# In block 2 and its FFN, h is made without 1/rms and the products are scaled on GpSimd

## The reference, cut to what matters

```
x = first_block(...)                      # ends: x = rmsnorm(x, final_norm_g)
h = x * rsqrt(mean(x*x) + 1e-6) * norm1_g
p = h @ w_in                              # columns: u 1024, v 1024, g 1024, x_lru 1024
u, v = gelu(p_u), layernorm(gelu(p_v))
y_gm = u * (tril(ws) @ v + bs)            # per chunk of 128 tokens and head
y_lru = rg_lru(causal_conv4(p_x)) * gelu(p_g)
x = x + concat(rmsnorm(y_gm), rmsnorm(y_lru)) @ w_out
h = x * rsqrt(mean(x*x) + 1e-6) * norm2_g
up = causal_conv3(h @ ffn_w_up)           # 2048 -> 12288 columns
x = x + (gelu(up_gate) * up_val) @ ffn_w_down
return rmsnorm(x, final_g)
```

## Time and profile before

| | us |
|---|---|
| median of 3 runs (lowest to highest) | 2453.39 (2450.84 to 2458.06) |
| the profiled execution | 2454.96 |
| its span | 2453.2 |
| mean granted clock of TensorE | 0.978 |
| TensorE, products busy | 2324.8 (95%) |
| VectorE busy | 1291.5 (53%) |
| ScalarE busy | 1043.2 (43%) |
| GpSimd busy | 197.1 (8%) |

### The profile page before, as it was taken

One profiled execution on the slowest core, in us unless ns is written; L12 is line 12 of the kernel. 1 busy time (PEld: TensorE's weight loads), 2 busy tenths in 40 slices (PEclk: granted clock), 3 DMA queues, 4 the chain that ended last, 5 costly groups with the idle time before them and its releaser, 6 DMA issues.

```text
span 2453.2 us, 30580 instructions
## 1 busy us (share of the span) xinstructions
PE 2324.8 (95%) x12135; PEld 1861.9 (76%) x12135; DVE 1291.5 (53%) x2110; ACT 1043.2 (43%) x1596; POOL 197.1 (8%) x237
## 2 busy tenths in 40 slices
PE   5889999999999979899989988989999999999998
PEld 2467777677777657678877867868888888888887
DVE  2444533142332263545666776557665676567664
ACT  2232333342321263445544545445543555345543
POOL 1000100000010131100021014120000000000001
PEclk8999999999999999999989999989999999999999
DMA  9864433335655565534555554646655655565652
GB/s 367 294 236 172 142 120 124 123 112 171 232 172 172 202 221 208 167 102 147 187 157 171 180 172 130 189 132 186 189 181 188 189 183 186 186 186 186 188 184 83
DMA packets 347021, 436.66 MB, mean 178 GB/s; under 512 B 13848, under 2 KB 269280, under 8 KB 345984
## 3 DMA queue, kind: packets, MB, share of 16 engines
q1 hardware_dynamic: 341376, 413.19, 51.8%
q0 software_dynamic: 3408, 16.38, 1.9%
q10 hardware_dynamic: 2096, 5.15, 0.6%
HBM read 428.37 MB, written 6.29 MB: 177 GB/s over the span
## 4 chain that ended last, share of the span: by engine, by line
PE 85%; DVE 5%; ACT 4%; DMA 3%; issue 2%; POOL 1%; SPq 0%; ACTq 0%; POOLq 0%; DVEq 0%
PE ps L1151 32%; PE ps L1152 16%; PE ps L1146 5%; PE ps L1148 5%; PE ps L1147 5%; PE ps L1132 4%; PE ps L1134 4%; PE ps L1133 4%; PE ps L1113 3%; ACT SPL L1329 2%; DVE SPL L1555 2%; PE ps L1196 1%; PE ps L1213 1%; DMA RAW<-in_w_in_dram 1%; DMA RAW<-in_ada_w_dram 1%
## 5 line engine op out<-in xcount | busy, mean ns | idle before, releaser
L1151 PE MATMUL ps<-HS,SPL 128*128 128x512 f32 x3456 | 1236.1, 402 | 16.9 <-POOL HS L2007 16.1
L1555 DVE TENSOR_TENSOR SPL<-RAW,SPL 128x1024 fp32r<-128x1024 f32 x592 | 726.4, 1233 | 669.4 <-ACT SPL L1329 667.3
L1152 PE MATMUL ps<-HS,SPL 128*128 128x256 f32 x3456 | 973.6, 282 | 0.0
L1329 ACT ACTIVATE SPL<-RAW 128x1024 fp32r<-128x1024 f32 x592 | 621.7, 1057 | 536.1 <-PE ps L1152 356.5
L1151 PEld LDWEIGHTS ps<-HS,SPL 128*128 128x128 f32 x3456 | 654.6, 189 | 183.4 <-POOL HS L2007 16.9
L1152 PEld LDWEIGHTS ps<-HS,SPL 128*128 128x128 f32 x3456 | 658.2, 190 | 2.1 <-issue 1.9
L1132 PE MATMUL ps<-SPL,HS 128*128 128x512 f32 x576 | 248.5, 431 | 30.1 <-ACT XT L1371 8.5
L1134 PE MATMUL ps<-SPL,HS 128*128 128x512 f32 x576 | 228.5, 397 | 0.0
L1133 PE MATMUL ps<-SPL,HS 128*128 128x512 f32 x576 | 228.4, 396 | 0.0
L1146 PE MATMUL ps<-HS,SPL 128*128 128x512 f32 x512 | 212.2, 414 | 1.2 <-DVE HS L1711 1.2
L1148 PE MATMUL ps<-HS,SPL 128*128 128x512 f32 x512 | 200.5, 392 | 0.0
(11 more groups left out here) (251 smaller groups left out, 1543.7 us busy)
## 6 DMA issues: line engine op xcount, KB each, us to landing
RAW<-in_w_in_dram SPq DMA_DIRECT2D x208, 512.0 KB, 5.6
RAW<-in_ada_w_dram SPq DMA_DIRECT2D x192, 512.0 KB, 4.9
RAW<-in_ffn_w_up_dram SPq DMA_DIRECT2D x192, 512.0 KB, 3.6
RAW<-in_w_out_dram SPq DMA_DIRECT2D x96, 512.0 KB, 4.5
RAW<-in_ffn_w_down_dram SPq DMA_DIRECT2D x96, 512.0 KB, 3.4
x_spill<-XT POOLq DMA_DIRECT2D x2, 2048.0 KB, 14.8
XT<-x_spill POOLq DMA_DIRECT2D x1, 4096.0 KB, 15.8
MM<-in_x_dram ACTq DMA_DIRECT2D x2, 1024.0 KB, 10.8
```

The source lines that it names most:

```text
L1151: mm(PS[b][:, :], wr, hh, start=k == 0, stop=False, skip_group_check=True)
L1152: m = mm(PS[b][:, 256:512], wl, hh[:, 0:256], start=False, stop=k == KT - 1, skip_group_check=True)
L1329: act(SPL[:, (n - 1) % NSPL, 0, :], raw_of(i), ACT.Copy).then_inc(s_hi, 1)
L1555: tt(w[:, 1, :], raw_of(s["i"]), w[:, 0, :].bitcast(F32), ALU.subtract).then_inc(s_lo, 1)
```

## The change

For the h of block 2 and of the FFN the 1/rms is left out. `bare_tile` takes the place of `split_tile`: two tiles are put into `hi` as soon as an out group has summed them, the high part by ScalarE from x times g, the low part by VectorE. The norm's steps become steps of `hi` during the first group of the next projection: `both_a` (count, means, power, diagonals), `both_b` (rows), `keep_rows`, which copies the rows into SBUF (RSB) and at the first seam two columns (VRS); `up_a`, `up_b`, `keep_rows` at the second. The planner pops `hi` until the rows are there (`kept`) before it puts the first join. After each join of u, x_lru, g and the FFN's up groups GpSimd multiplies the two joined tiles by RSB (`join_scale`), and the consumer waits for that; the Gelu of v takes 1/rms as its scale per token. `keep_x` waits for the tile of h made from the same x. The product of the two channel weights (`gain_both`) is made ahead of layer 2's out projection.

```diff
@@ join
-        def join(outs, banks, done):
+        def join(outs, banks, done, rows=None):
             s = put("join", outs=outs, banks=banks, last=done)
             ready = [(s_jd, 2 * s["n"] - 1), (s_jd, 2 * s["n"])]
             for b, r in zip(banks, ready):
                 bank_last[b] = [r]
+            if rows is None:
+                return ready
+            z = put("join_scale", outs=outs, ready=ready, rows=rows)
+            y["rows_read"] = (s_js, 2 * z["n"])
+            return [(s_js, 2 * z["n"] - 1), (s_js, 2 * z["n"])]
+
+        def bare_tile(k, src, g, dst, ready, done, last):
+            z = {}
+            def s0():
+                z["n"] = put("bare_hi", src=src, g=g, dst=dst, last=[ready, *last])["n"]
+            def s1():
+                done[k] = (s_bl, put("bare_lo", src=src, g=g, dst=dst, hi=z["n"])["n"])
+            return [s0, s1]
+
+        def made(done):
+            def ready(k):
+                while k not in done:
+                    hi.pop(0)()
+                return [done[k]]
             return ready
+
+        def keep_rows(ready, after):
+            s = put("keep_rows", last=[ready, *after])
+            bank_last[5] = [(s_rsb, s["n"])]
+            y["rows"] = (s_rsb, s["n"])
+
+        def kept():
+            while "rows" not in y:
+                hi.pop(0)()
+            return y["rows"]
@@ x_out (layer 2); x_add the same with "if squares is sq2"
+                    if not both:
+                        hi.extend(staged([y["tile"](j0 + i, (s_res, n + i)) for i in range(2)]))
@@ u_out; xlru_out, g_out and up_out the same
-                ready = join([UU[:, j0 + i, :] for i in range(2)], banks, [multiplied(), y["ended"]])
+                ready = join([UU[:, j0 + i, :] for i in range(2)], banks, [multiplied(), y["ended"]], kept())
@@ first seam
-        y["ended"] = add_up1(marks[4])
...
-        need["in2"] = on_demand([split_tile("in", k, XV[:, 0, k, :], GG[:, k, :], RS0, HH[0][:, k, :, :], lambda: [(s_bnr, 1), (s_gg1, 1)],
-                                            done, [y["ended"]]) for k in range(KT)], done)
-        need["in2"](1)
+        put("gain_both")
+        done_in = {}
+        read_in = multiplied()
+        y["tile"] = lambda k, ready: bare_tile(k, XV[:, 0, k, :], GG[:, k, :], HH[0][:, k, :, :], ready, done_in, [read_in, (s_gg1, 1)])
+        run_chunks(marks[4])
+        y["ended"] = multiplied()
...
+        need["in2"] = made(done_in)
         put("lru_maps_in", last=[y["ended"]])
-        hi.extend([idle] * 2 + [keep_x(k) for k in range(KT)] + [lambda: put("decay")])
+        hi.extend([both_a, idle, both_b, lambda: keep_rows((s_bnr, 1), [])] + [keep_x(k) for k in range(KT)] + [lambda: put("decay")])
@@ second seam
-        flush(hi)
         y["down"] = multiplied()
...
+        hi.extend([up_a, idle, up_b, lambda: keep_rows(y["up_rows"], [read])])
@@ ScalarE
+                    act(s["dst"][:, 0, :], s["src"], ACT.Copy, scale=s["g"]).then_inc(s_bh, 1)
...
-                        act(VN[:, t, s["g"] * 512:(s["g"] + 1) * 512], PS[b][:, :], ACT.Gelu_apprx_tanh).then_inc(s_vc, 1)
+                        act(VN[:, t, s["g"] * 512:(s["g"] + 1) * 512], PS[b][:, :], ACT.Gelu_apprx_tanh, scale=VRS[:, t:t + 1]).then_inc(s_vc, 1)
@@ VectorE
+                elif kind == "bare_lo":
+                    e.wait_ge(s_bh, s["hi"])
+                    stt(s["dst"][:, 1, :], s["src"], s["g"], s["dst"][:, 0, :].bitcast(F32), ALU.mult, ALU.subtract).then_inc(s_bl, 1)
+                elif kind == "keep_rows":
...
+                    if n == 1:
+                        copy(VRS, RSTD[:, 2:4])
+                    copy(RSB, RS0).then_inc(s_rsb, 1)
@@ GpSimd
+                elif kind == "join_scale":
...
+                    for o, (sm, v) in zip(s["outs"], s["ready"]):
+                        e.wait_ge(sm, v)
+                        tt(o, o, RSB, ALU.mult).then_inc(s_js, 1)
```

More of the change, by code:

```diff
@@ L794, in f @@
             def f():
-                need["in2"](k)
-                s = put("keep_x", k=k, last=[(s_bnr, 2)])
+                s = put("keep_x", k=k, last=[(s_bnr, 2), done_in[k]])
                 bank_last[4] = [(s_kx, s["n"])]
@@ L810, in f @@
                 pads = (s_z, s["n"])
-                ready = join([T(a)[:, 3:259], T(b)[:, 3:259]], banks, [multiplied(), *la, *lb])
+                ready = join([T(a)[:, 3:259], T(b)[:, 3:259]], banks, [multiplied(), *la, *lb], kept())
                 z = {}
@@ L852, in f @@
             def f():
-                s = put("v_gelu", g=g, banks=banks, last=[multiplied()])
+                s = put("v_gelu", g=g, banks=banks, last=[multiplied(), kept()])
                 for i, b in enumerate(banks):
@@ L882, in f @@
                 xs = [T(slot)[:, 0:256], T(slot)[:, 256:512]]
-                ready = join(xs, banks, [multiplied(), *last])
+                ready = join(xs, banks, [multiplied(), *last], kept())
                 def mul():
@@ L901, in f @@
                         squares.add(XV[:, 0, j0 + i, :], j0 + i, (s_res, n + i))
+                if squares is sq2:
+                    hi.extend(staged([y["tile"](j0 + i, (s_res, n + i)) for i in range(2)]))
             return f
@@ L911, in f @@
                 cs = [c0, (c0 + 1) % 8]
-                ready = join([CV[c][:, 2:258] for c in cs], banks, [multiplied(), (s_pad, 1), *conv_last[cs[0]], *conv_last[cs[1]]])
+                ready = join([CV[c][:, 2:258] for c in cs], banks, [multiplied(), (s_pad, 1), *conv_last[cs[0]], *conv_last[cs[1]]], kept())
                 ks = (2 * i, 2 * i + 1)
@@ L1000, in two_block_program, with both_a, both_b @@
         project1(marks[3])
-        y["ended"] = add_up1(marks[4])
[L1004 to L1010, removed]
-        need["in2"] = on_demand([split_tile("in", k, XV[:, 0, k, :], GG[:, k, :], RS0, HH[0][:, k, :, :], lambda: [(s_bnr, 1), (s_gg1, 1)],
-                                            done, [y["ended"]]) for k in range(KT)], done)
-        need["in2"](1)
+        put("gain_both")
[4 more added lines that the diff above has]
+        y["ended"] = multiplied()
+        def both_a():
+            sq1.count(6)
+            cnt = sq1f.count(6, 2)
+            y["both_slot"], last = take()
+            y["power"] = tick("power")
+            put("both_norms", slot=y["both_slot"], last=[cnt, *last], power=y["power"])
+            bank_last[6] = [(s_bn, 1)]
+        def both_b():
+            put("both_rows", slot=y["both_slot"], after=use(4, 5))
+            give(y["both_slot"], (s_bnr, 2))
+        need["in2"] = made(done_in)
         put("lru_maps_in", last=[y["ended"]])
-        hi.extend([idle] * 2 + [keep_x(k) for k in range(KT)] + [lambda: put("decay")])
+        hi.extend([both_a, idle, both_b, lambda: keep_rows((s_bnr, 1), [])] + [keep_x(k) for k in range(KT)] + [lambda: put("decay")])
         run_chunks(marks[5])
@@ L1044, in two_block_program, with up_a, up_b @@
         run_chunks(marks[8])
-        flush(hi)
         y["down"] = multiplied()
-        cnt = sq2.count(4)
-        slot, bank_last[4] = rstd_a(2, 1.0 / D, PS[4][:, 0:2], [cnt])[0], [(s_ms, count["rstd_a"])]
-        rs2 = rstd_b(2, slot, 5)
-        done2 = {}
-        need["up"] = on_demand([split_tile("up", k, XV[:, 0, k, :], V(c_n2 + k), RS0, HH[0][:, k, :, :], lambda: [rs2], done2, [y["down"]]) for k in range(KT)], done2)
-        need["up"](1)
+        need["up"] = made(done_up)
+        def up_a():
+            cnt = sq2.count(4)
+            y["up_slot"], bank_last[4] = rstd_a(2, 1.0 / D, PS[4][:, 0:2], [cnt])[0], [(s_ms, count["rstd_a"])]
+        def up_b():
+            y["up_rows"] = rstd_b(2, y["up_slot"], 5)
+        read = y["rows_read"]
+        del y["rows"]
+        hi.extend([up_a, idle, up_b, lambda: keep_rows(y["up_rows"], [read])])
         put("conv_pads", last=[y["down"]])
@@ L1463, in scalar @@
                     act(a, s["src"], ACT.Square, scale=1.0 if s["col"] is None else V(s["col"])).then_inc(s_sqa, 1)
+                elif kind == "bare_hi":
+                    for sm, v in new(*s["last"]):
+                        e.wait_ge(sm, v)
+                    act(s["dst"][:, 0, :], s["src"], ACT.Copy, scale=s["g"]).then_inc(s_bh, 1)
                 elif kind == "y1":
```

21 lines of the change are left out of this document (16 added, 5 removed).

## The result

| | before | after |
|---|---|---|
| median of the runs of this comparison (lowest to highest) | 2452.64 (2450.84 to 2458.06) | 2427.71 (2421.36 to 2431.43) |
| the profiled execution, its span | 2454.96, 2453.2 | 2428.89, 2427.1 |
| mean granted clock of TensorE | 0.978 | 0.978 |
| GpSimd busy | 197.1 | 249.5 |

The account below looks back on a forecast made before the run. TensorE carries 85% of the chain of waits, so gains lie where it idles or runs at its lower clock: two seams. 35.3 - 3.2 - 2.4 - 1.2 - 0.3 = 28.2 us gained, predicting 2425 us, range 2416 to 2438.

Parts of the forecast that it names:

- Item 1: Seams into block 2 and the FFN: tiles made early, statistics covered, gain 18.4 and 16.9, together 35.3 us.
- margin of 0.1 us: Seam 1, under chunk 3: the diagonals need 2.7 us against 2.77, just hidden; uncovered they cost up to 2.4.
- Item 2: GpSimd multiplies 120 tiles at 0.74 us, 89 us off TensorE; only latency can cost, 0.7 to 2.9 us per pair.
- Item 3: Ends of the three up rounds: late multiplies delay taps and then TensorE, cost 3.2 us, bounds 0 and 8.7.
- Item 4: Seam 1's side queue slips one step: extra Exp load and late mask at v, 2.4 us, bounds 0 and 4.
- Item 5: Last g pair: a multiply delays the sum of squares and the count, cost 1.2 us, bounds 0 and 4.
- Everything hides: Rival: GpSimd's multiply fits into gaps counted as packed, so its latency costs nothing; 2419 us, chance 0.15.
- The statistics don't hide: Rival, at the seams: waits for count and row sums return, about 8 us less gain; 2433 us, chance 0.07.
- GpSimd taxes VectorE in all up groups: Rival: collisions leak 0.3 us in each of 48 groups, 14 us; 2439 us, chance 0.12.
- Slower: Rival, up groups: ScalarE's first tap waits for GpSimd, weight splits come late, TensorE stops; 2480 us, chance 0.04.
- 5.7 us of slack per split: Up groups: ScalarE's split is ready 5.7 us before its chunk, against at most 2.9 of added latency.

Follow-up runs that it names:

- no_slip: Changed kernel with seam 1's side queue three steps shorter (no idle, keep_x 12 to 15 in pairs); 2420.06 us, ratio 0.9874.
- stats_first: Changed kernel with all steps of the norm ahead of the next group's first chunk at both seams, tiles still early; 2432.10 us, ratio 0.9906.
- seam2_only: Changed kernel with block 2 as before, so only the FFN's h is made without 1/rms; 2438.70 us, ratio 0.9930.
- ffn_triple: Changed kernel with two useless GpSimd operations (rows added, then subtracted) ahead of each FFN multiply; 2512.83 us, ratio 1.0251.
- second profile of after: The changed kernel timed and profiled once more, nothing edited; 2422.09 us, ratio 0.9872.
- late_count: Changed kernel with the count of y's norm one chunk later in the second out projection; 2420.63 us, ratio 0.9872.
- ffn_double: Changed kernel with one useless GpSimd addition of the rows ahead of each FFN multiply; 2447.90 us, ratio 0.9972.
- both_edits: Changed kernel with the edits of late_count and no_slip together; 2427.47 us, ratio 0.9887.

## Why the prediction was right

**Item 1, the seams (18.4 + 16.9 = 35.3 forecast).** Measured 18.7 + 16.9 = 35.6. The gaps went, the clock stayed at 1.00, and the margin of 0.1 us that I gave the diagonals at seam 1 held; at seam 2 0.17 us of waiting is left. This is the whole gain, and its mechanism is as forecast.

**Item 2, the multiply.** One multiply takes 0.65 us on average in the FFN, where I took 0.74. GpSimd's busy time grew by 52 us and not by 89, as I left out that the low parts of 32 tiles go from GpSimd to VectorE.

**Item 3, the ends of the up rounds (+3.2 forecast, 0 to 8.7).** Measured +1.1: TensorE waits 0.70, 0.53 and 0.71 instead of 0.15, where I forecast 0.9 to 1.6. At the first end (answers to the earlier trace rows), VectorE, ScalarE, GpSimd, TensorE:

```profile
1780.67 0.76 DVE L1751 TENSOR_TENSOR MM<-ps,MM 128x256 f32<-128x256 f32 x2 [0.81 <-ACT MM L1492]
1781.89 1.60 DVE L1614 TENSOR_TENSOR SPL<-RAW,SPL 128x1024 fp32r<-128x1024 f32 x1 [0.47 <-ACT SPL L1383]
1783.41 1.66 DVE L1980 SCALAR_TENSOR_TENSOR MM<-MM,VV 128x256 f32<-128x256 f32 x4
...
1782.51 1.10 ACT L1578 ACTIVATE MM<-MM,VV 128x256 f32<-128x256 f32 x2 [0.65 <-POOL MM L2081]
...
1781.17 1.24 POOL L2081 TENSOR_TENSOR MM<-MM,GX 128x256 f32<-128x256 f32 x2 [9.85 <-DVE MM L1751]
...
1789.93 0.50 PE L1205 MATMUL ps<-HS,SPL 128*128 128x512 f32 x1 [0.70 <-DVE HS L1993]
```

GpSimd's two multiplies take 0.62 each where I took 0.73 from its sums, and the first starts beside the second join. The split begins 0.52 us before the second multiply ends and takes 1.60 instead of 1.23. That 0.37 is the whole delay of VectorE's taps: they start 2.74 us behind the join instead of 2.37. The tap on ScalarE is later by more (1.84 instead of 1.08 behind the join), but it is not what the end waits for. I had the split and VectorE's taps end behind the whole second multiply, +0.7 to +1.4; that is the step that was mis-sized, and it came out cheaper.

The Trainium skill (SBUF — State Buffer, "Who interferes with whom") lets a VectorE instruction with one SBUF input run freely beside GpSimd, and excludes one with two. The trace agrees with the first half: the second join (one operand in PSUM) overlaps the first multiply from 1781.17 to 1781.43 and the pair of joins keeps its 0.76 us, as before. With the second half it agrees in direction: the split is stretched, by 0.37 of the 0.52 us for which its record overlaps that of the multiply. The prediction held no row for the first half.

**Item 4, the side queue (+2.4 forecast).** Measured +2.6 in the v groups, with one table load more than before (8 instead of 7 between 1330 and 1520 us) and the wait on v's turn at 2.65 instead of 0.48; both are gone in no_slip and in stats_first, which don't slip. Right, mechanism and size.

**Item 5, the g groups and the second out projection (+1.2 forecast, 0 to 4).** Measured -0.3 + 7.2 = +6.9: the term that was mis-sized, beyond its bound. TensorE's waits in the opening grew by 3.0: 0.32 for a split, 2.07 for the count, 0.6 more at a tile of y. Of the count's 2.07, 0.61 stands in seam2_only too; the other 1.46 (two multiplies at 0.73) is near the 1.2 that I took. The rest of the step, 4.2 us, is products at the lower clock (window at 0.86). That part is not fixed by the code: ffn_triple has the same instructions up to there and the same wait (2.06), and its step is 3.3, with 0.95 in the same window; the second profile of after has 7.2 and 0.86 again, and the other kernels with seam 1 changed have 2.7 to 3.5 at 0.90 to 0.95. What decides how far the clock falls there is not shown. I had priced waits there at the full clock.

**What the sum hid.** The terms of the change add up to 35.6 - 1.1 - 2.6 - 6.9 - 0.3 (x_lru) = 24.7, 3.5 less than my 28.2. The rest of the ledger has nothing to do with the change: +5.8 upstream, and three stretches where only the period of TensorE's pairs differs between the two profiles, +1.0 in u and x_lru, +1.3 in the second out projection and -9.5 in the FFN. In seam2_only, where u's code is that of before, u drifts in the same way, and its out projection doesn't. Together they leave 1.4 us in the change's favour. That the forecast of the sum (2425 against 2427.71 and 2422.09) was nearer than that of its terms is in part luck: item 3 came out cheaper, item 5 dearer.

**The rivals.** "Everything hides" (2419, a ratio of 0.986) gives a time that the second comparison of the change doesn't exclude, nor those of late_count and no_slip, but the trace of after shows waits of 2.65, 2.07 and 1.9. "The statistics don't hide": no wait at the seams. "GpSimd taxes VectorE in all up groups": splits are slower by 0.09 us on average, and no TensorE wait comes of it. "Slower": its mechanism is real and needs two more operations per tile to be worse than before. My ground against it, 5.7 us of slack per split, was no bound: at 4.2 us of ScalarE's wait per group TensorE already begins to wait for splits, and at 5.7 it stops for 1.5 to 2.3 us in about every second group. The bound is ScalarE's own idle time in a group.

## What to carry to other kernels

A factor per token can leave the operand and go onto the product if the rows are there before the first result is evicted; the worth is the waits at the seam plus the time that TensorE then spends at its lower clock. Here it was 35.6 us at two seams, 15 of them from covering the statistics and the rest from making the tiles early. The slack of an in-order engine is the time it waits for the engine that it feeds, in the same loop body: read it from the idle column of its groups, and add a chain's collisions to its durations. Extra waits where TensorE already waits can cost more than themselves: 3.0 us of them cost 7.2 in both profiles of after, and about their own length (2.6 to 3.0 us cost 2.8 to 3.5) in kernels with the same code up to there or nearly so.

## What the runs showed of the hardware that was not expected

A pair of products (512 and 256 columns) at a granted clock of 1.00 has one of two periods, 0.347 or 0.353 us, constant over long stretches. In the thirteen traces it changes about 110 times, some 90 of them where TensorE had just stood idle and 10 behind the gate products of x_lru; 8, all in ffn_double and ffn_triple, show neither. Both periods stand in the rows of before: 11.09 us from eviction to eviction in the projection, 11.31 in the FFN, which I had taken for a property of the two stages. It isn't one. The same up groups in two kernels whose FFN instructions are the same, no_slip and then both_edits: ScalarE's evictions of two groups, and TensorE's records of 1850 to 1890 (count: durations in ns, least, median, most; first and last start):

```profile
1878.14 0.66 ACT L1492 ACTIVATE MM<-ps 128x256 f32<-128x256 f32 x2 [1.65 <-PE ps L1206]
1889.23 0.66 ACT L1492 ACTIVATE MM<-ps 128x256 f32<-128x256 f32 x2 [1.65 <-PE ps L1206]
...
L1205 PE MATMUL ps<-HS,SPL x116: 392/394/395, 1849.9 to 1889.7; 128*128 128x512 f32 x116
```

```profile
1881.56 0.66 ACT L1492 ACTIVATE MM<-ps 128x256 f32<-128x256 f32 x2 [1.71 <-PE ps L1206]
1892.85 0.66 ACT L1492 ACTIVATE MM<-ps 128x256 f32<-128x256 f32 x2 [1.70 <-PE ps L1206]
...
L1205 PE MATMUL ps<-HS,SPL x114: 395/398/403, 1849.9 to 1889.8; 128*128 128x512 f32 x114
```

11.09 against 11.29 us a group. From the end of the first up group to the last product, before takes 803.7 us, both_edits 803.4, after 795.2, no_slip and late_count 793.5; the second profile of after takes 798.4 where the first took 795.2. That is 3 us between two executions of one kernel and 10 us between kernels with the same FFN, more than any of the small edits is worth. It accounts for the profiled execution of both_edits, which saves the most waits and took no less time. What sets the period was not found; no experiment here forced it.
